# One 8 KB gather of both expert rows per slot, in place of two 4 KB gathers, in a decoder layer on one core

## The chip, the cores and the metric

The kernel runs on one core of a Trainium2 chip. The metric is the device time of one execution, in microseconds (us). Five engines of the core work side by side, each through its own instruction list in order: TensorE (PE, with its weight loads PEld), VectorE (DVE), ScalarE (ACT), GpSimd (POOL) and SyncE (SP). They wait for each other by semaphores. Sixteen DMA engines move data for transfers that the engines issue.

## What is computed

The reference is one layer of a decoder, for a prompt of 512 tokens and 8 sample tokens: three attention branches, their merge, and then a mixer of experts with product keys. The change lies in this mixer. Each token has 8 heads with 16 experts each, thus 128 slots. An expert is one row of 1024 numbers (4 KB) in each of two tables:

```
u = u_tab[e_idx]                    # (tokens, 128, 1024)
v = v_tab[e_idx]
a = gelu(einsum('tsd,td->ts', u, x)) * gate
y = h + einsum('ts,tsd->td', a, v)
```

The indices `e_idx` and the gates come from the retrieval, a search by scores.

## The kernel before

The 512 prompt tokens are 4 tiles of 128 tokens, a token per partition. The mixer (`mix_prompt`) runs over 4 x 128 = 512 slots; in a slot every partition needs the rows of its own expert. For slot s of tile t:

- POOL issues an indirect DMA of 128 rows of `u_tab` (L3190), 4 KB each, in all 0.5 MB, into one of six buffers. It waits till the product of slot s-6 is done.
- VectorE multiplies the row with the token and sums it up (L3219: two instructions, the product and a short read of the accumulator), into `ex_dots`.
- ScalarE takes the GELU of 16 slots at once (L3267, 128x16). VectorE multiplies 16 of them with the gates (L3226).
- POOL issues the rows of `v_tab` (L3199) 21 steps behind, into one of six other buffers. It waits till slot s-6 of these is used up.
- The row times the coefficient is added to y 24 steps behind (`LAG`), in one of two ways that `adds_on_vector` lays down by slot: on VectorE (L3235), or on TensorE (L3292) as a matmul with a diagonal matrix that ScalarE makes (L3262).

The rest of the layer runs beside these slots. A planner of fixed numbers (`RETRIEVE_HALF` to `MEMORY`, class `Beside`) spreads each stage evenly over a range of slot steps, on every engine: at step s an engine first issues what is due of the side stage, then its part of the slots. The stages are the retrieval for the other tiles (steps 0 to 62), the merge of the last two tiles (62 to 106), its output projection and norm (to 147), retrieval of the last tiles (to 211), weights (to 217), the compression of the sample cache (COMPRESS, 217 to 289, 256 loads `cs_ch` of 128 KB issued by SP), index and selection (to 353), then the attention of the samples with gathers by POOL (L2147, `da_kv`, `da_bias`, `sl_kv`, `sl_bias`), and the memory attention. Order and place are thus fixed; only the time at which a step comes moves. After the prompt block `expert_samples` does the same mixing for the 8 sample tokens, in 8 chunks of 128 rows (L3346 gathers, L3435 products, L3365 matmuls).

Of the kernel before, what the change touches and what calls it, by code (L numbers as in the profile page):

```python
# [15 lines left out]
P = 128  # L16
D = 1024
# [208 lines left out]
class Kernel:  # L226
# [1024 lines left out]
    def compress_samples(self, wts):  # L1251
# [7 lines left out]
        with tmp:  # L1259
# [43 lines left out]
            with self.block(COMPRESS) as block:  # L1303
# [113 lines left out]
                def _(dve):  # L1417
# [3 lines left out]
                    mix_done, acc_done = self.mix_sems[3][4:6]  # L1421
                    _, dve_upto, pe_upto = v_counts()
                    dve.wait_ge(mix_done, pe_upto[V_MOVES - 1])
                    dve.wait_ge(acc_done, dve_upto[V_MOVES - 1])
# [1242 lines left out]
    def finish_rows(self, tag, x_t, o_t, rows, load_x, h, xf, save=(), ahead=False, extra=(), early=False):  # L2667
# [5 lines left out]
        with tmp:  # L2673
# [22 lines left out]
            def turn(name, dst):  # L2696
                self.transposes(f"{tag}_{name}", [(dst[:, 4 * q:4 * q + 4, P * t:P * t + r], [mixed[:r, t, P * k:P * k + P] for k in range(4 * q, 4 * q + 4)])
                                                  for t, r in enumerate(rows) for q in range(2)])


            also = [(h[:r, t, :], load_x[t]) for t, r in enumerate(rows)] + list(extra)
# [4 lines left out]
            turn("mixed", t_view)  # L2706
# [4 lines left out]
            self.linear(f"{tag}_pq", t_view, rows, i["w_pq"], D, mixed, also=save, loaded=pq_w)  # L2711
# [7 lines left out]
    def finish_prompt(self, tag, t0, t1, h, o_t):  # L2719

        self.finish_rows(tag, self.xT[:, :, P * t0:P * t1], o_t, ROWS[t0:t1], self.xs[t0:t1], h, self.xf_prompt[:, t0:t1],
                         save=[(self.s["h"][P * t0:P * t1].rearrange("(t p) d -> p t d", p=P), h)], early=t0 == 0)
# [6 lines left out]
    def prompt_experts(self):  # L2729

        ctx = ExitStack()
        with ctx:
# [18 lines left out]

            u = lambda n: u_new[:, n % NU_BUF] if n % NU_BUF < NU_BUF // 2 else u_old[:, n % NU_BUF - NU_BUF // 2]
            work = ExitStack()
            with work:
# [3 lines left out]
                self.mix_sems = ([self.sem(f"ex_u_in{n}") for n in range(NU_BUF)], [self.sem(f"ex_v_in{n}") for n in range(NV_BUF)],  # L2758
                                 [self.sem(f"ex_h_in{n}") for n in range(2)],
# [6 lines left out]
            with work:  # L2766
                h = self.sb("fq_h", [P, TP - FIRST_TILES, D], F32, work)
                self.finish_prompt("fq", FIRST_TILES, TP, h[:], self.o_rest[:])
# [13 lines left out]
            self.mix_prompt(idx, gate, dots, coef, u=u, v=v, x=lambda t: self.xf_prompt[:, t], y=lambda t: y[:, t % 2], diag=diag, y_ps=y_ps,  # L2782
# [372 lines left out]
    def mix_prompt(self, idx, gate, dots, coef, u, v, x, y, diag, y_ps, chosen, beside, merged):  # L3155
# [4 lines left out]
        u_in, v_in, h_in, (dot_done, gelu_done, coef_done, diag_done, mix_done, acc_done, y_done) = self.mix_sems  # L3160
# [348 lines left out]
```

## Time and profile before

| what | us |
|---|---|
| median of three runs | 3009.91 (3000.89 to 3014.22) |
| span of the profiled execution, its first to its last instruction | 3030.2 |
| mixing of the prompt, first to last product | 812.8 to about 2832 |
| last addition into y of the prompt | 2893.9 |
| sample experts, first gather to the end | 2993.1 to 3030.2 |

Beside the span no other time is listed for the profiled execution; its span is 20.3 us above the median. The stages of the mixing phase, by the slot steps above, lie in the trace as: steps 0 to 41 from 812.8 to 923.3 us, 42 to 61 to 993.4, merge to 1189.8, projection and norm to 1347.5, compression 1566.9 to 1912.6, attention of the samples from 2170.1 (95 products to 2589.1), sliding-window attention of the samples to about 2830. The mixing takes two thirds of the time, and no engine is busy over more than 60% of the whole, so it is read by stage.

### The profile page before, as it was taken

The numbers are of one execution on the slowest core, as the hardware profiler recorded it, in microseconds if no ns is written. First come the engines' busy times: TensorE is split into PE (matmuls) and PEld (weight loads), VectorE is DVE, ScalarE is ACT, GpSimd is POOL, SyncE is SP. The second block draws the span as 40 slices with busy tenths as digits, with TensorE's granted clock in tenths as the row PEclk, the third lists the DMA queues.
The fourth block names the chain that finished last, engine by engine and source line by source line (L and its number), as shares of the span: only waits on it lengthen the run. The fifth ranks groups of instructions, "written<-read, shape, count | busy, mean of one in ns | idle before, by whom it ended". The sixth has DMA issues, their size and how long they took to land. (4 is left out here: it accounts for less than half of the span.)

```text
span 3030.2 us, 26401 instructions
## 1 busy us (share of the span) xinstructions
PE 1823.4 (60%) x7749; PEld 1077.9 (36%) x7749; DVE 1804.8 (60%) x3991; ACT 391.4 (13%) x994; POOL 1371.8 (45%) x1331
## 2 busy tenths in 40 slices
PE   7999796998145696456615645676212231655575
PEld 3475664544122232222204433552112221444521
DVE  4344556311688666679986656678566646766513
ACT  2010464301010001101100111111000010110000
POOL 1000242100267445567775443656567776755302
PEclk9999798999579798778967777558655555555577
DMA  4031400342389988999999997888678779977753
GB/s 137 23 115 37 169 2 1 111 153 104 111 283 351 361 323 288 330 356 354 338 348 370 335 328 274 310 287 314 198 242 316 255 248 339 344 272 279 278 211 112
DMA packets 273785, 727.80 MB, mean 240 GB/s; under 512 B 47881, under 2 KB 91426, under 8 KB 273066
## 3 DMA queue, kind: packets, MB, share of 16 engines
q0 software_dynamic: 156672, 564.61, 51.9%
q1 hardware_dynamic: 115802, 157.28, 15.0%
q10 hardware_dynamic: 1168, 4.23, 0.4%
q8 instruction: 62, 1.02, 0.1%
q14 instruction: 81, 0.66, 0.1%
HBM read 717.42 MB, written 12.66 MB: 241 GB/s over the span
## 5 line engine op out<-in xcount | busy, mean ns | idle before, releaser
L3199 POOL DMA_INDIRECT branch_rows_t<-in_v_tab,e_idx x437 | 519.8, 1190 | 400.5 <-DVE heads_t L3235 269.7
L3190 POOL DMA_INDIRECT ex_u<-in_u_tab,e_idx x257 | 279.0, 1086 | 350.2 <-POOLq L3093 246.7
L3235 DVE SCALAR_TENSOR_TENSOR heads_t<-branch_rows_t,ex_coef,heads_t 128x1024 f32<-128x1024 f32 x333 | 427.3, 1283 | 3.3 <-DVE me_lt L2648 0.3
L3219 DVE CUSTOM_DVE_ANT_0 ex_u<-ex_u,heads_t 128x1024 f32<-128x1024 f32 x257 | 314.1, 1223 | 168.8 <-DMA ex_u<-in_u_tab,e_idx 153.7
L3219 DVE CUSTOM_DVE_ANT_0 heads_t<-heads_t 128x1024 f32<-128x1024 f32 x255 | 311.9, 1224 | 132.2 <-DMA heads_t<-in_u_tab,e_idx 116.4
L3190 POOL DMA_INDIRECT heads_t<-in_u_tab,e_idx x255 | 276.1, 1083 | 88.5 <-issue 75.8
L3292 PE MATMUL ex_y_ps<-branch_rows_t,heads_t 128*128 128x512 f32 x416 | 215.3, 653 | 115.3 <-DMA branch_rows_t<-in_v_tab,e_idx 51.1
L1335 PE MATMUL cs_pp<-cs_ch,xn_t 128*128 128x256 f32 x512 | 139.0, 439 | 192.6 <-DMA cs_ch<-in_cache_cmp_kv 192.6
L818 PE MATMUL in_acc<-in_w,xn_t 128*128 128x512 f32 (+7 forms) x560 | 208.8, 529 | 6.0 <-POOLq L176 4.5
L1335 PEld LDWEIGHTS cs_pp<-cs_ch,xn_t 128*128 128x128 f32 x512 | 113.2, 224 | 220.5 <-DMA cs_ch<-in_cache_cmp_kv 142.8
L3292 PEld LDWEIGHTS ex_y_ps<-branch_rows_t,heads_t 128*128 128x128 f32 x416 | 79.0, 205 | 244.1 <-issue 173.2
L818 PEld LDWEIGHTS in_acc<-in_w,xn_t 128*128 128x128 f32 (+1 forms) x560 | 96.0, 176 | 108.9 <-issue 88.6
L1843 POOL IOTA heads_t<- 128x32 int32 x1 | 0.2, 164 | 223.1 <-SPq L175 223.1
L1936 PE MATMUL sl_at_lt_ps<-sample_q_t,sl_at_kt 64*128 64x4 f32 x256 | 64.8, 357 | 59.5 <-issue 44.8
L1636 PE MATMUL at_t_ps<-at_diag,at_exp 128*128 128x128 f32 (+3 forms) x608 | 87.4, 288 | 21.9 <-POOL at_diag L1724 21.1
L3199 POOL DMA_INDIRECT cmp_k_t<-in_v_tab,e_idx x50 | 61.9, 1237 | 73.9 <-DVE heads_t L3235 56.9
L3267 ACT ACTIVATE ex_coef<-ex_dots 128x16 f32<-128x16 f32 x32 | 6.9, 216 | 663.3 <-DVE ex_dots L3219 566.8
L1936 PEld LDWEIGHTS sl_at_lt_ps<-sample_q_t,sl_at_kt 64*128 64x128 f32 x256 | 59.2, 319 | 85.0 <-issue 69.3
L2865 PE MATMUL fq_mg_g_ps<-fq_mg_wg,xn_t 128*128 128x512 f32 x192 | 85.0, 595 | 0.0
L1636 PEld LDWEIGHTS at_t_ps<-at_diag,at_exp 128*128 128x128 f32 (+3 forms) x608 | 71.8, 185 | 34.8 <-POOL at_diag L1724 22.3
L1722 POOL TENSOR_SCALAR at_diag<-ident,at_sum,branch_gates 128x128 f32<-128x128 f32 x96 | 42.0, 447 | 74.4 <-DVE at_sum L1762 68.7
L1678 ACT ACTIVATE at_exp<-at_logits,at_max 128x128 f32<-128x128 f32 (+7 forms) x128 | 63.0, 493 | 65.1 <-DVE at_max L1750 63.9
(715 smaller groups left out, 3190.8 us busy)
## 6 DMA issues: line engine op xcount, KB each, us to landing
cs_ch<-in_cache_cmp_kv SPq DMA_DIRECT2D x256, 128.0 KB
fq_mg_wg<-in_w_gate SPq DMA_DIRECT2D x6, 2048.0 KB, 18.3
in_w<-in_w_in SPq DMA_DIRECT2D x4, 2048.0 KB
branch_rows_t<-in_v_tab,e_idx POOLq DMA_INDIRECT x437
first_w<-in_w_gate SPq DMA_DIRECT2D x3, 2048.0 KB, 7.9
fp_wb<-in_w_branch SPq DMA_DIRECT2D x6, 1024.0 KB, 10.2
fp_wg<-in_w_gate SPq DMA_DIRECT2D x3, 2048.0 KB, 8.1
fq_mg_wb<-in_w_branch SPq DMA_DIRECT2D x6, 1024.0 KB, 22.0
```

The source lines that it names most:

```text
L818: last = pe.matmul(acc[:r, u % 2, :n], self.xT[:, k, P * t:P * t + r], w[:, j % 2, k, :n], start=(k == 0), stop=(k == KD - 1))
L1335: last = pe.matmul(pp[:, n % 2, 256 * c:256 * c + 256].rearrange("p (g k m) -> p g k m", g=KV, m=8), wts[:, c, r, :], ch[:, n % NBUF, :, c ...
L1636: last = pe.matmul(t_ps[:w, u % 2, k, :], ex[:, u % 6, P * k:P * k + w], diag[:, u % 4, :], start=True, stop=True)
L1678: act.activation(ex[:, u % 6, :keys(u)], src[:, u % 4, :keys(u)], ACT.Exp, bias=mx[:, u:u + 1], scale=scale, accum_out=sm[:, u:u + 1]).the ...
L1722: pool.tensor_scalar(d, ident[:], r, self.g_nsa[:, t, k:k + 1], ALU.mult, ALU.mult).then_inc(scaled, 1)
L1936: last = pe.matmul(ltv[:m, g, j, b, :], lhs, q, start=True, stop=True)
L2865: last = pe.matmul(g_ps[:r, u % 2, :], xT[:, k, cols], wg[j % depth][:, k, :], start=(k == 0), stop=(k == KD - 1))
L3190: pool.indirect_dma_start(out=u(s), out_offset=None, in_=i["u_tab"], in_offset=bass.IndirectOffsetOnAxis(ap=idx[:, t, m:m + 1], axis=0)).t ...
L3199: pool.indirect_dma_start(out=v(n), out_offset=None, in_=i["v_tab"], in_offset=bass.IndirectOffsetOnAxis(ap=idx[:, t, m:m + 1], axis=0)).t ...
L3219: dve.tensor_tensor_reduce(out=u(s), in0=u(s), in1=x(t), scale=1.0, scalar=0.0, op0=ALU.mult, op1=ALU.add, accum_out=dots[:, t, m:m + 1]). ...
L3235: dve.scalar_tensor_tensor(out=y(t), in0=v(n), scalar=coef[:, t, m:m + 1], in1=y(t), op0=ALU.mult, op1=ALU.add).then_inc(acc_done, 1)
L3292: last = pe.matmul(y_ps[:, q, :], diag[:, (pe_upto[n] - 1) % 8], v(n)[:, 512 * q:512 * q + 512], start=n in first_pe, stop=n in last_pe)
```

## The change

Both tables become one, `uv_tab`, a row of 8 KB: 1024 numbers of u, then 1024 of v. The host puts them side by side. A slot has one gather of 128 rows of 8 KB, 1 MB (L3201 after), into one of seven buffers of 8 KB; it waits till slot s-7 has both its product and its addition. The lag of the additions falls from 24 steps to 3. ScalarE makes the coefficient slot by slot at the next step: a GELU of 128x1 (L3257), a wait for itself, a copy scaled by the gate (L3259), and for TensorE's slots the diagonal matrix. VectorE's product with the gates is gone. VectorE takes first the addition of slot s-3, then the product of slot s. As the rule in `adds_on_vector` goes by step, other slots fall to TensorE: 162 where it was 134, and 350 to VectorE where it was 378. The residual rows `fq_h` of the merged tiles, whose place is needed, are loaded between merge and projection. The sample experts have 8 gathers of 8 KB rows instead of 8 and 8.

```diff
-V_MOVES = 150
-NU_BUF = NV_BUF = 6
-CHUNK, LAG, AHEAD, SETTLE, RELOAD = 16, 24, 3, 4, 30
+ROW_MOVES = 172
+NBUF, NDIAG = 7, 4
+LAG, SETTLE, RELOAD = 3, 4, 30
...
+            old_pairs = self.heads_space(TP * D + 2 * D, [2, 2 * D])
+            diag = self.heads_space(TP * D + 6 * D, [NDIAG, P])
+            new_pairs = self.sb("ex_pairs", [P, 2, 2 * D], F32, ctx)
...
-                        if s >= NU_BUF:
-                            pool.wait_ge(dot_done, s - NU_BUF + 1)
-                        pool.indirect_dma_start(out=u(s), out_offset=None, in_=i["u_tab"],
-                                                in_offset=bass.IndirectOffsetOnAxis(ap=idx[:, t, m:m + 1], axis=0)).then_inc(u_in[s % NU_BUF], 16)
-                    n = s - LAG + AHEAD
...
-                        if n >= NV_BUF:
-                            mixed(pool, n - NV_BUF)
-                        pool.indirect_dma_start(out=v(n), out_offset=None, in_=i["v_tab"],
...
+                        if s >= NBUF:
+                            pool.wait_ge(dot_done, s - NBUF + 1)
+                            if by_dve[s - NBUF]:
+                                pool.wait_ge(acc_done, dve_upto[s - NBUF])
+                            else:
+                                pool.wait_ge(mix_done, pe_upto[s - NBUF])
+                        pool.indirect_dma_start(out=pair(s), out_offset=None, in_=i["uv_tab"],
+                                                in_offset=bass.IndirectOffsetOnAxis(ap=idx[:, t, m:m + 1], axis=0)).then_inc(pair_in[s % NBUF], 16)
...
-                    c = s - 3 - CHUNK
-                    if c >= 0 and c % CHUNK == 0 and c < NS:
-                        t, m = at(c)
-                        dve.wait_ge(gelu_done, c // CHUNK + 1)
-                        w = coef[:, t, m:m + CHUNK]
-                        dve.tensor_tensor(w, w, gate[:, t, m:m + CHUNK], ALU.mult).then_inc(coef_done, 1)
...
-                    n = s - LAG + AHEAD
-                    if 0 <= n < NS and not by_dve[n]:
...
-                    if s % CHUNK == CHUNK - 1 and s < NS:
...
+                    n = s - 1
+                    if 0 <= n < NS:
+                        t, m = at(n)
+                        c = coef[:, t, m:m + 1]
+                        act.wait_ge(dot_done, n + 1)
+                        act.activation(c, dots[:, t, m:m + 1], ACT.Gelu_apprx_tanh).then_inc(gelu_done, 1)
+                        act.wait_ge(gelu_done, n + 1)
+                        act.activation(c, c, ACT.Copy, scale=gate[:, t, m:m + 1]).then_inc(coef_done, 1)
+                        if not by_dve[n]:
+                            act.wait_ge(coef_done, n + 1)
+                            if pe_upto[n] > NDIAG:
+                                act.wait_ge(mix_done, pe_upto[n] - NDIAG)
+                            act.activation(diag[:, (pe_upto[n] - 1) % NDIAG], ident[:], ACT.Copy, scale=c).then_inc(diag_done, 1)
...
-                    for dst, table, sems in ((u, i["u_tab"], u_in), (rows, i["v_tab"], v_in)):
-                        for n in range(N):
-                            pool.indirect_dma_start(out=dst[:, n], out_offset=None, in_=table,
+                    for n in range(N):
+                        pool.indirect_dma_start(out=pairs[:, n], out_offset=None, in_=i["uv_tab"],
```

In the fence the pieces stand in the order of POOL, VectorE and ScalarE in `mix_prompt`, then POOL in `expert_samples`.

How the order moves shows at three places. First POOL, where the attention of the samples gathers its biases (`da_bias`); `ex_u`, `heads_t`, `branch_rows_t` and `ex_pairs` are places of the row buffers. Before:

```order
L3199 DMA branch_rows_t<-in_v_tab,e_idx 128x1024
L2147 DMA da_bias<-tmp_bias_pos,da_past_ix 128x16
L3190 DMA ex_u<-in_u_tab,e_idx 128x1024
L3199 DMA branch_rows_t<-in_v_tab,e_idx 128x1024
L2147 DMA da_bias<-tmp_bias_pos,da_past_ix 128x16
```

And after:

```order
L2147 DMA da_bias<-tmp_bias_pos,da_past_ix 128x16
L3201 DMA branch_rows_t<-in_uv_tab,e_idx 128x2048
L2147 DMA da_bias<-tmp_bias_pos,da_past_ix 128x16
L3201 DMA ex_pairs<-in_uv_tab,e_idx 128x2048
L2147 DMA da_bias<-tmp_bias_pos,da_past_ix 128x16
```

Where POOL issued two gathers of rows and one of biases to a step, it issues one and one.

Then ScalarE where the sliding-window attention copies its transposed keys (`sl_at_kt`, L1999) out of TensorE's memory. Before:

```order
L1999 COPY da_at_kt<-da_at_kt_ps 64x256 x3
L3267 ACT_TABLE_LOAD
L3267 ACTIVATE ex_coef<-ex_dots 128x16
L1999 COPY da_at_kt<-da_at_kt_ps 64x256 x13
L2002 ACT_TABLE_LOAD
L2002 ACTIVATE da_at_p,da_at_sm<-da_at_p,da_at_mx 64x264
L3267 ACT_TABLE_LOAD
L3267 ACTIVATE ex_coef<-ex_dots 128x16 x2
L1999 COPY sl_at_kt<-sl_at_kt_ps 64x256 x25
L3267 ACTIVATE ex_coef<-ex_dots 128x16
```

And after:

```order
L1999 COPY sl_at_kt<-sl_at_kt_ps 64x256
L3257 ACTIVATE ex_coef<-ex_dots 128x1
L3259 ACTIVATE ex_coef<-ex_coef,e_gate 128x1
L1999 COPY sl_at_kt<-sl_at_kt_ps 64x256 x2
L3257 ACTIVATE ex_coef<-ex_dots 128x1
L3259 ACTIVATE ex_coef<-ex_coef,e_gate 128x1
L1999 COPY sl_at_kt<-sl_at_kt_ps 64x256 x2
```

Up to 25 copies stood between two GELUs of 16 slots; now one or two copies stand between the coefficients of neighbouring slots.

Third, ScalarE in the compression, where `cs_hid` (L1395) waits for a matmul of TensorE. Before:

```order
L3267 ACTIVATE ex_coef<-ex_dots 128x16
L1322 COPY cs_part<-cs_pp 128x2x128 x2
L1395 ACTIVATE cs_hid<-cs_hp,cmp_peh 128x2x255
L1322 COPY cs_part<-cs_pp 128x2x128 x2
L1400 ACT_TABLE_LOAD
```

And after:

```order
L3257 ACTIVATE ex_coef<-ex_dots 128x1
L3259 ACTIVATE ex_coef<-ex_coef,e_gate 128x1
L1395 ACTIVATE cs_hid<-cs_hp,cmp_peh 128x2x255
L3257 ACTIVATE ex_coef<-ex_dots 128x1
L3259 ACTIVATE ex_coef<-ex_coef,e_gate 128x1
L3257 ACTIVATE ex_coef<-ex_dots 128x1
L3259 ACTIVATE ex_coef<-ex_coef,e_gate 128x1
L1322 COPY cs_part<-cs_pp 128x2x128 x2
```

Behind the waiting `cs_hid` stood coefficients that were up to 8 steps away from their use; now those of the next slot stand there.

## Rows read from the trace of the kernel before

**Rows 1.** the page's fifth part (groups of instructions), whole execution.
```profile
L3199 POOL DMA_INDIRECT branch_rows_t<-in_v_tab,e_idx x437 | 519.8, 1190 | 400.5 <-DVE heads_t L3235 269.7
...
L3235 DVE SCALAR_TENSOR_TENSOR heads_t<-branch_rows_t,ex_coef,heads_t 128x1024 f32<-128x1024 f32 x333 | 427.3, 1283 | 3.3 <-DVE me_lt L2648 0.3
L3219 DVE CUSTOM_DVE_ANT_0 ex_u<-ex_u,heads_t 128x1024 f32<-128x1024 f32 x257 | 314.1, 1223 | 168.8 <-DMA ex_u<-in_u_tab,e_idx 153.7
L3219 DVE CUSTOM_DVE_ANT_0 heads_t<-heads_t 128x1024 f32<-128x1024 f32 x255 | 311.9, 1224 | 132.2 <-DMA heads_t<-in_u_tab,e_idx 116.4
```

**Rows 2.** busy us (count) of PE, PEld, DVE, ACT, POOL; clock, DMA, GB/s.
```profile
812.80:923.30 110.50, 45.48 (x116) 19.36 (x116) 93.27 (x310) 14.27 (x36) 80.19 (x64) 0.71 0.85 299
923.30:993.40 70.10, 34.87 (x69) 12.28 (x68) 60.04 (x139) 5.14 (x14) 51.74 (x43) 0.88 0.92 331
993.40:1189.80 196.40, 171.51 (x400) 64.41 (x400) 118.33 (x155) 20.20 (x29) 90.30 (x85) 0.93 0.89 326
1189.80:1347.50 157.70, 71.92 (x199) 35.57 (x200) 108.45 (x142) 15.15 (x29) 96.11 (x86) 0.70 0.95 352
1566.90:1912.60 345.70, 169.47 (x676) 132.34 (x676) 209.22 (x369) 35.37 (x56) 165.53 (x150) 0.74 0.89 323
2170.10:2589.10 419.00, 92.08 (x800) 76.26 (x801) 254.29 (x402) 17.58 (x37) 296.71 (x271) 0.50 0.81 276
2589.10:2680.20 91.10, 53.04 (x207) 37.89 (x206) 77.99 (x99) 12.18 (x34) 70.93 (x65) 0.50 0.98 368
```

**Rows 3.** the same view, VectorE's product line L3219 alone.
```profile
812.80:923.30 110.50, 51.26 (x84) 0.71 0.85 299
...
2170.10:2589.10 419.00, 117.36 (x191) 0.50 0.81 276
```

**Rows 4.** POOL's groups of instructions, 2170.1 to 2589.1 us.
```profile
L3199 POOL DMA_INDIRECT branch_rows_t<-in_v_tab,e_idx x96 | 118.4, 1233 | 41.7 <-issue 28.1 <-DVE heads_t L3235 13.6
L3190 POOL DMA_INDIRECT heads_t<-in_u_tab,e_idx x48 | 49.6, 1033 | 14.6 <-issue 14.6
L3190 POOL DMA_INDIRECT ex_u<-in_u_tab,e_idx x49 | 48.0, 980 | 21.3 <-issue 21.3
```

**Rows 5.** VectorE's waits in it: us in total, times, longest.
```profile
DVE heads_t L3219 <- DMA heads_t<-in_u_tab,e_idx: 74.5, 38, 12.0
DVE ex_u L3219 <- DMA ex_u<-in_u_tab,e_idx: 67.1, 37, 5.3
```

**Rows 6.** queues, 1603 to 1621 us: packets, MB, share of 16 engines.
```profile
q0 software_dynamic: 1559, 5.68, 80.7%
q1 hardware_dynamic: 1559, 1.42, 23.0%
```

**Rows 7.** the same, 2811 to 2830 us.
```profile
q1 hardware_dynamic: 240, 6.82, 83.2%
q0 software_dynamic: 265, 1.01, 13.0%
```

**Rows 8.** the same, 1850 to 1856 us.
```profile
q1 hardware_dynamic: 880, 0.80, 43.8%
```

**Rows 9.** waits, 806 to 2880 us, VectorE's and ScalarE's.
```profile
DVE cs_part L1322 <- PE cs_pp L1335: 90.7, 8, 15.7
...
DVE ex_coef L3226 <- ACT ex_coef L3267: 20.5, 1, 20.5
...
ACT cs_hid L1395 <- PE cs_hp L1346: 155.4, 8, 27.4
...
ACT fq_mg_sig L2887 <- PE fq_mg_g_ps L2865: 87.7, 12, 9.7
```

**Rows 10.** the timeline at the end (start us, us).
```profile
2993.05 0.94 POOL L3346 DMA_INDIRECT es_u<-in_u_tab,es_idx  x1 [17.09 <-DVE es_idx L3426]
...
3011.39 15.27 PE L3365 MATMUL es_y_ps<-es_rows,es_diag 128*8 128x512 f32 x32 [25.08 <-ACT es_diag L3381]
```

**Rows 11.** the timeline of VectorE at 2893 us.
```profile
2893.46 0.19 DVE L2665 COPY sample_o_t<-me_o_ps 128x32 f32<-128x32 f32 x1 [20.35 <-PE me_o_ps L2633]
```

More of the change, by code:

```diff
@@ L2665, in _, with finish_rows @@
                     c.link(dve.tensor_copy(self.o8_t[:, 8:12, :], ov))
-    def finish_rows(self, tag, x_t, o_t, rows, load_x, h, xf, save=(), ahead=False, extra=(), early=False):
+    def finish_rows(self, tag, x_t, o_t, rows, load_x, h, xf, save=None, ahead=False, extra=(), early=False, late=False):
         nt, i = len(rows), self.i
@@ L2694, in finish_rows, with turn @@
             mixed = self.sb(f"{tag}_mixed", [P, nt, D], F32, tmp)
-            def turn(name, dst):
+            def turn(name, dst, store=None):
                 self.transposes(f"{tag}_{name}", [(dst[:, 4 * q:4 * q + 4, P * t:P * t + r], [mixed[:r, t, P * k:P * k + P] for k in range(4 * q, 4 * q + 4)])
-                                                  for t, r in enumerate(rows) for q in range(2)])
-            also = [(h[:r, t, :], load_x[t]) for t, r in enumerate(rows)] + list(extra)
+                                                  for t, r in enumerate(rows) for q in range(2)], store=store)
+            also = ([] if late else [(h[:r, t, :], load_x[t]) for t, r in enumerate(rows)]) + list(extra)
             if ahead:
@@ L2705, in finish_rows, with load_h @@
                 self.merge(tag, x_t, o_t, rows, mixed, also, weights=weights, after=after, samples=not early)
-            turn("mixed", t_view)
+            load_h = None
+            if late:
+                h, h_in = self.sb(f"{tag}_h", [P, nt, D], F32, tmp)[:], self.sem(f"{tag}_h_in")
+                def load_h(sp):
+                    for t, r in enumerate(rows):
+                        sp.dma_start(h[:r, t, :], load_x[t]).then_inc(h_in, 16)
+                    sp.wait_ge(h_in, 16 * nt)
+            turn("mixed", t_view, load_h)
             self.linear(f"{tag}_out", t_view, rows, i["w_out"], D, h, add=h, loaded=out_w, ahead=then)
@@ L2766, in prompt_experts @@
             with work:
-                h = self.sb("fq_h", [P, TP - FIRST_TILES, D], F32, work)
-                self.finish_prompt("fq", FIRST_TILES, TP, h[:], self.o_rest[:])
+                self.finish_prompt("fq", FIRST_TILES, TP, None, self.o_rest[:], late=True)
             self.recycle()
@@ L3331, in expert_samples @@
             y_ps = self.ps("es_y_ps", [P, 2, 512], ctx)
-            u_in = [self.sem(f"es_u_in{n}") for n in range(N)]
-            v_in = [self.sem(f"es_v_in{n}") for n in range(N)]
+            pair_in = [self.sem(f"es_pair_in{n}") for n in range(N)]
             stored = self.stores("y_sample")
@@ L3362, in _ @@
                         pe.wait_ge(diag_done, n + 1)
-                        pe.wait_ge(v_in[n], 16)
+                        pe.wait_ge(pair_in[n], 16)
                         for a in range(2):
-                            last = pe.matmul(y_ps[:DB, a, :], diag[:, n, :], rows[:, n, 512 * a:512 * a + 512], start=(n == 0), stop=(n == N - 1))
+                            last = pe.matmul(y_ps[:DB, a, :], diag[:, n, :], pairs[:, n, D + 512 * a:D + 512 * a + 512], start=(n == 0), stop=(n == N - 1))
                     last.then_inc(mix_done, 1)
@@ L3474 @@
     for name in _INS:
+        if name == "v_tab":
+            continue
+        if name == "u_tab":
+            put("uv_tab", _np.concatenate([_np.asarray(inputs["u_tab"]), _np.asarray(inputs["v_tab"])], axis=1))
+            continue
         a = _np.ascontiguousarray(inputs[name])
```

84 lines of the change are left out of this document (34 added, 50 removed).

## The prediction

> **What bounds the kernel now.** I read the groups of instructions first. VectorE's products wait for their rows: 153.7 us in one group of buffers and 116.4 in the other [rows 1], 270 us together, a tenth of the span. POOL's v gathers wait most for VectorE's additions, 269.7 us; that is a full ring, not a shortage. So the question is what makes the u rows late, and the busy shares by stretch answer it differently by stage [rows 2]:
>
> - Steps 0 to 61 (812.8 to 993.4 us): VectorE is busy 93.27 of 110.5 and 60.04 of 70.1 us, with the retrieval between its products. VectorE bounds.
> - Merge (993.4 to 1189.8): TensorE 171.51 of 196.4 us. TensorE bounds.
> - Projection and norm (1189.8 to 1347.5) and 2589.1 to 2680.2: the DMA engines at 0.95 and 0.98, 352 and 368 GB/s. Bytes bound.
> - Compression (1566.9 to 1912.6): nobody is over 0.89; VectorE waits 90.7 us for `cs_pp` [rows 9], and that waits for the 128 KB loads.
> - 2170.1 to 2589.1: DMA only at 0.81 and 276 GB/s, VectorE 254.29 of 419 us, POOL 296.71 in 271 instructions. Here stand 74.5 + 67.1 = 141.6 us of the 270 [rows 5]. POOL's own groups show idle time put down to "issue" behind nearly every gather, 14.6 us for 48 and 21.3 for 49 [rows 4]: with some 0.3 us between 271 instructions, about 80 us, and 296.71 busy, POOL is occupied 378 of 419 us. POOL bounds, by the number of its gathers.
>
> **The change part by part.** The sum is made against the profiled span of 3030.2 us, which lies 20.3 us above the median of the runs; I take the same 20.3 off at the end.
>
> *POOL in the attention of the samples.* Each of 97 steps loses a u gather: 49.6 + 48.0 busy and 14.6 + 21.3 of issue gaps [rows 4] = 133 us of POOL. The row that remains is priced as a v gather now, 1233 ns, since it too is one descriptor list of 128 rows. POOL would then need 419 - 133 = 286 us. VectorE needs 254.29 plus its waits for others than rows, so at least 254. The bytes stay: 419 us at 276 GB/s [rows 2] are 115.6 MB, which take 314 us at 368 GB/s, the best rate of a long stretch [rows 2], or 293 us at 7.10 MB in 18 us = 394 GB/s, the best of a short one [rows 6]. So the DMA is next, and the gain is at most 127 us and at least nothing. The mean rate of the four stretches at 0.89 or more [rows 2] is (326 + 352 + 323 + 368) / 4 = 342; that is where this kernel arrives when it asks for all it can. 115.6 / 0.342 = 338: **-81**.
>
> The Trainium skill (DMA: Bandwidth & Descriptors, section Anatomy of one DMA — SWDGE (gpsimd) path) fits a transfer from POOL as some 2.0 us plus its bytes at 436 GB/s, and its section Bandwidth advises at least 1 MiB. By that, two 0.5 MB transfers cost 6.4 us and one of 1 MB 4.4, an estimate from that page; it would give 2 us for every slot wherever rows are waited for. The rows that are gathered now speak against this here: with 0.5 MB gathers the engines already reach 0.98 and 368 GB/s [rows 2], so this start is covered by transfers in flight.
>
> *Head.* A product needed 0.5 MB; now it needs its whole pair. Up to 923.3 us 84 / 2 = 42 products ran (the count takes in the reads of the accumulator) [rows 3], and only 18 v rows were due, so 110.5 us at 299 GB/s = 33 MB sufficed. Now 42 pairs are 42 x 1.05 = 44 MB, and at 350 GB/s (the projection's 352 [rows 2]) that takes 126 us: **+16**. Bounds: nothing (394 GB/s would give 112) to +37 (at 299). The next 20 steps need 21 MB, 60 us, under VectorE's 70: nothing. In the merge, TensorE's slots are added no faster and no slower; its bound stays: nothing, bounds -5 to +10 for the packets that weights now queue with.
>
> *Longer packets.* From the two windows a packet costs a + b x bytes: 1559 packets of 3.64 KB in 0.807 x 16 x 18 us = 149 ns [rows 6], 240 of 28.4 KB in 0.832 x 16 x 19 us = 1054 ns [rows 7]. So b = 0.0365 ns per byte and a = 16 ns; a pair in one packet saves 16 of 298 ns, 5%, at most (window 6 counts 103.9% in all, so the true a is smaller). I take 3% on 157.7 + 91.1 = 249 us [rows 2]: **-8**, bounds 0 to -13.
>
> *Compression.* It is fed by 256 loads of 128 KB in 1 KB pieces. Beside gathers both queues moved 1559 packets each [rows 6]: one of theirs for one of the others', 1.42 MB in 18 us = 79 GB/s for `cs_ch`, and 133 GB/s when alone [rows 8]. With pieces of 8 KB against 1 KB the same turn gives it 1 part in 9, about 44 GB/s. 256 x 131 KB = 33.6 MB at 44 GB/s would take 763 us, but only while a gather is under way; the total of bytes is the same, and the ring holds the gathers back when VectorE waits. One bound is nothing. For the other: between 79 and 44 GB/s a load of 131 KB takes 1.7 or 3.0 us, 1.3 more; if a sixth of the 256 are met when they are waited for, 54 us. I take the lower end's neighbourhood, as VectorE's wait for `cs_pp` is only 90.7 us in 8: **+10**.
>
> *ScalarE and the short lag.* The gate product leaves VectorE: 32 short instructions, inside a stretch where it waits anyway: nothing. Two small activations per slot come to ScalarE, each at most the 0.2 us or so of other rows: 0.4 of a slot that lasts 2.8 us or more, at ACT busy 17.58 of 419 [rows 2]. The coefficient is now due two steps later instead of eight or more. Against it stands one gain: VectorE waited 20.5 us for the GELU that stood behind 25 copies [rows 9]; a stage that waits for its transposed keys will keep half: **-10**, bounds -20 to 0. Additions: 28 move from VectorE to TensorE at 1283 ns [rows 1], but 24 of all stood behind the last product, where the end is set by the memory attention: `me_o_ps` is what VectorE waits 20.35 us for at 2893.46 [rows 11]. Shorter tail: nothing.
>
> *Sample experts.* TensorE's 32 matmuls take 15.27 us from 3011.39 [rows 10] and need the coefficients of all 8 products. Eight pairs of 1.05 MB from 2993.05 + 2 at 350 GB/s land at 3019, where eight u rows sufficed before: the end moves by some 10 us: **+10**, bounds +4 to +14.
>
> Sum: -81 + 16 - 8 + 10 - 10 + 10 = **-63**, so 2967 in the profile and 3009.9 - 63 = 2947, say **2945** in the runs.
>
> **The rivals.**
>
> *B, ScalarE in lockstep (slower).* ScalarE waits for TensorE in its side stages: 155.4 us in 8 for `cs_hp`, 87.7 in 12 for the merge's gates [rows 9]. Before, a coefficient behind such a wait had 8 steps; now VectorE's additions have two steps, about 5 us, then VectorE stops, so does the ring, and TensorE's next work for VectorE is late too. It decides from 78 us on, the 63 of the gain and the 15 that a measurement needs. If 15 us of each of the 8 waits fall on VectorE, 120 are lost: 3009.9 - 63 + 120 = about 3067. Against it: VectorE waits in the same stage for the same TensorE already (90.7), and ScalarE's waits are partly its running ahead. Chance 0.14.
>
> *C, queues share badly (no change).* Weights of merge and projection, `cs_ch` and the samples' rows queue in turn with 8 KB packets; +54 in the compression instead of 10 and +10 in the merge, so 2945 + 54 = about 3000. Chance 0.12.
>
> *D, POOL's price grows with the row.* If 128 rows of 8 KB cost POOL twice the 1233 ns, the gain of 81 goes: 3009.9 - 63 + 81 = 3028. No row has such a gather; that POOL writes one list entry for each row, whatever its length, is my assumption, and v and u rows of one length differ by 0.2 us already [rows 4]. Chance 0.05.
>
> *E, the fixed start of a transfer.* Each row wait was the start of a transfer, and a transfer fewer gives nearly all 270 us back, less the head and the end: 3010 - 270 + 16 + 10 = about 2766. The section cited above would have it so. Chance 0.06.
>
> **How the numbers follow.** My own case has 0.63; its own range is 2901 to 2991, from the largest bound taken alone on either side (-127 for -81, +54 for +10). With E below and B above, each cut off in part, the range of 8 in 10 is 2893 to 3032: it leaves out most of E and most of B. Faster, by over 0.5% (what a measurement of this kernel can tell from no change; under 2995): my case, E and 0.03 of C, 0.72. Within: 0.09 of C and 0.03 of D, 0.12. Slower: B and 0.02 of D, 0.16.
>
> **What the changed profile would show.** The POOL line of gathers near 1.2 us each in the stretch with `da_bias`, the stretch at 340 to 370 GB/s and about 340 us instead of 419, product waits there under 60 us. The 42nd product about 16 us later after the first. `cs_pp` waits some 10 us longer. Few waits of VectorE's addition for L3259; many over 5 us mean B. A gather of 2.4 us on POOL means D. The prediction is wrong if the stretch from 2170 on stays at 276 GB/s, or if additions wait for coefficients by over 60 us in all.

## The result, and the profile after

The changed kernel takes 2871.69 us (median of 4 runs, 2866.79 to 2881.74) where the kernel before took 3012.06 in the same rounds. The ratio is 0.957, with a 95% interval of 0.951 to 0.963. The forecast was 2945, with a range of 2893 to 3032. It is faster by 140 us, twice the 65 that I had given it, and outside the range.

The profiled span is 2873.5 us against 3030.2, so 157 us less. That is 17 more than the medians differ by, since the profiled execution of before lies above its median; in which stages these 17 stand can't be told. A second profile of the changed kernel (experiment 12) has each stage within 6 us of the one shown, but for the compression (356.6 us). The time between the starts of two products gives it by stage. The forecast beside it is that of my sum:

| steps | what runs beside | before, us | after, us | change | forecast |
|---|---|---|---|---|---|
| 0 to 62 | retrieval | 180.6 | 178.8 | -2 | +16 |
| 62 to 106 | merge | 196.4 | 207.5 | +11 | 0 |
| 106 to 147 | projection, norm | 157.7 | 166.5 | +9 | -5 |
| 147 to 217 | retrieval, last | 219.3 | 210.4 | -9 | 0 |
| 217 to 289 | compression | 345.7 | 347.4 | +2 | +10 |
| 289 to 353 | index, selection | 257.6 | 230.7 | -27 | 0 |
| 353 to 448 | attention of the samples | 418.9 | 330.3 | -89 | -81 |
| 448 to 480 | sliding window, first part | 91.1 | 81.0 | -10 | -3 |
| 480 to 511 | sliding window, second part | 150.7 | 103.8 | -47 | -10 |
| from 511 on | memory attention, sample experts | 199.4 | 203.4 | +4 | +10 |

The groups of instructions of the page after, which answer to [rows 1]:

```profile
L3201 POOL DMA_INDIRECT ex_pairs<-in_uv_tab,e_idx x147 | 188.4, 1281 | 543.1 <-POOLq L3099 244.1
L3201 POOL DMA_INDIRECT branch_rows_t<-in_uv_tab,e_idx x171 | 210.1, 1229 | 283.3 <-DVE heads_t L3226 183.7
...
L3231 DVE CUSTOM_DVE_ANT_0 branch_rows_t<-branch_rows_t,heads_t 128x1024 f32<-128x1024 f32 x171 | 208.8, 1222 | 58.9 <-DMA branch_rows_t<-in_uv_tab,e_idx 55.5
...
L3231 DVE CUSTOM_DVE_ANT_0 ex_pairs<-ex_pairs,heads_t 128x1024 f32<-128x1024 f32 x147 | 179.8, 1223 | 47.1 <-DMA ex_pairs<-in_uv_tab,e_idx 44.7
L3231 DVE CUSTOM_DVE_ANT_0 heads_t<-heads_t 128x1024 f32<-128x1024 f32 x146 | 178.1, 1221 | 42.0 <-DMA heads_t<-in_uv_tab,e_idx 39.2
...
L3259 ACT ACTIVATE ex_coef<-ex_coef,e_gate 128x1 f32<-128x1 f32 x512 | 150.8, 294 | 16.6
```

A gather of 8 KB rows takes POOL 1229 to 1281 ns, where a v gather of 4 KB rows took 1190. The products wait 55.5 + 44.7 + 39.2 = 139 us for their rows in these three groups, where it was 270. The stretches, with the columns of [rows 2]:

```profile
813.60:929.20 115.60, 85.55 (x197) 33.47 (x198) 94.94 (x309) 42.62 (x133) 62.75 (x41) 0.91 0.93 382
929.20:992.40 63.20, 38.24 (x72) 13.25 (x71) 60.52 (x139) 19.65 (x60) 29.95 (x19) 0.86 0.88 360
992.40:1199.90 207.50, 171.21 (x400) 64.38 (x400) 117.42 (x153) 62.06 (x131) 51.18 (x44) 0.91 0.81 313
1199.90:1366.50 166.60, 72.51 (x198) 35.70 (x199) 105.75 (x141) 35.55 (x110) 47.44 (x41) 0.69 0.85 331
1576.80:1924.20 347.40, 165.86 (x676) 129.05 (x676) 207.09 (x365) 67.73 (x194) 95.94 (x79) 0.74 0.86 322
2155.00:2485.30 330.30, 81.98 (x803) 67.85 (x804) 251.80 (x396) 62.27 (x222) 192.43 (x174) 0.51 0.91 350
2485.30:2566.30 81.00, 75.67 (x299) 55.08 (x299) 77.70 (x97) 29.30 (x113) 41.98 (x32) 0.50 1.01 420
```

From 2155 to 2485 us POOL is busy 192 us in 174 instructions, where it was 297 in 271; VectorE fills 252 of 330 us, and the bytes flow at 350 GB/s instead of 276. From 2485 to 2566 VectorE is busy 77.7 and TensorE 75.7 of 81 us, and the DMA engines are full at 420 GB/s: three limits lie close together there now (experiment 8 takes the bytes away and leaves 75). In the merge TensorE still needs 171 us, and the stretch is 11 us longer. POOL's gathers from 2155 to 2485 us, as in [rows 4]:

```profile
L3201 POOL DMA_INDIRECT branch_rows_t<-in_uv_tab,e_idx x41 | 46.1, 1123 | 51.6 <-DVE heads_t L3226 25.9 <-DVE ex_dots L3231 17.2 <-issue 8.5
L3201 POOL DMA_INDIRECT ex_pairs<-in_uv_tab,e_idx x28 | 33.6, 1201 | 15.6 <-DVE heads_t L3226 8.9 <-issue 6.4 <-DVE ex_dots L3231 0.3
L3201 POOL DMA_INDIRECT heads_t<-in_uv_tab,e_idx x28 | 32.1, 1145 | 24.9 <-DVE heads_t L3226 18.0 <-issue 6.9
```

97 gathers, 1123 to 1201 ns each, and most of the idle time before them, 70 of 92 us, is now the full ring (VectorE's addition or product), no longer "issue". Three waits of VectorE over the mixing, as in [rows 9]:

```profile
DVE cs_part L1322 <- PE cs_pp L1335: 66.8, 7, 17.6
...
DVE cmp_v L1432 <- PE cs_op L1358: 31.2, 4, 21.1
...
DVE heads_t L3226 <- ACT ex_coef L3259: 3.7, 12, 0.3
```

The addition waited 3.7 us in all for a coefficient. In the compression the wait for `cs_pp` is shorter than before (90.7) and that for `cs_op` longer (2.3 before). At the end, the first gather of the sample experts and TensorE's last matmuls, as in [rows 10]:

```profile
2827.20 0.95 POOL L3341 DMA_INDIRECT es_pairs<-in_uv_tab,es_idx  x1 [17.34 <-DVE es_idx L3421]
```

```profile
2853.20 16.72 PE L3360 MATMUL es_y_ps<-es_pairs,es_diag 128*8 128x512 f32 x32 [32.73 <-ACT es_diag L3376]
```

From the first gather to the end it is 46.3 us, where it was 37.2.

### The profile page after: what moved, and what is told of

Read it like the earlier page. It is cut to its first block and busy times, and to the rows that moved or that the text cites. A ratio compares the mean times of both kernels' runs of the same rounds, so it can differ in the third digit from the quotient of the medians.

```text
span 2873.5 us, 27584 instructions
## 1 busy us (share of the span) xinstructions
PE 1869.8 (65%) x7861; PEld 1083.5 (38%) x7861; DVE 1762.6 (61%) x3931; ACT 673.3 (23%) x2034; POOL 845.4 (29%) x811
## 5 line engine op out<-in xcount | busy, mean ns | idle before, releaser
L3257 ACT ACTIVATE ex_coef<-ex_dots 128x1 f32<-128x1 f32 x512 | 103.5, 202 | 1124.4 <-DVE ex_dots L3231 1006.4
L3201 POOL DMA_INDIRECT ex_pairs<-in_uv_tab,e_idx x147 | 188.4, 1281 | 543.1 <-POOLq L3099 244.1
L3201 POOL DMA_INDIRECT branch_rows_t<-in_uv_tab,e_idx x171 | 210.1, 1229 | 283.3 <-DVE heads_t L3226 183.7
L3201 POOL DMA_INDIRECT heads_t<-in_uv_tab,e_idx x146 | 183.5, 1257 | 284.8 <-DVE heads_t L3226 182.9
L3231 DVE CUSTOM_DVE_ANT_0 branch_rows_t<-branch_rows_t,heads_t 128x1024 f32<-128x1024 f32 x171 | 208.8, 1222 | 58.9 <-DMA branch_rows_t<-in_uv_tab,e_idx 55.5
L3231 DVE CUSTOM_DVE_ANT_0 ex_pairs<-ex_pairs,heads_t 128x1024 f32<-128x1024 f32 x147 | 179.8, 1223 | 47.1 <-DMA ex_pairs<-in_uv_tab,e_idx 44.7
L3231 DVE CUSTOM_DVE_ANT_0 heads_t<-heads_t 128x1024 f32<-128x1024 f32 x146 | 178.1, 1221 | 42.0 <-DMA heads_t<-in_uv_tab,e_idx 39.2
L3226 DVE SCALAR_TENSOR_TENSOR heads_t<-branch_rows_t,ex_coef,heads_t 128x1024 f32<-128x1024 f32 x126 | 161.6, 1282 | 10.8 <-DMA is_w<-tmp_w 5.6
L3259 ACT ACTIVATE ex_coef<-ex_coef,e_gate 128x1 f32<-128x1 f32 x512 | 150.8, 294 | 16.6
L3226 DVE SCALAR_TENSOR_TENSOR heads_t<-heads_t,ex_coef 128x1024 f32<-128x1024 f32 x100 | 128.1, 1281 | 27.5 <-issue 23.4
L3226 DVE SCALAR_TENSOR_TENSOR heads_t<-ex_pairs,ex_coef,heads_t 128x1024 f32<-128x1024 f32 x100 | 128.1, 1281 | 5.1 <-DMA fq_ffn_gain<-in_ln_ffn 0.9
L3289 PEld LDWEIGHTS ex_y_ps<-ex_pairs,heads_t 128*128 128x128 f32 x188 | 37.3, 215 | 150.3 <-ACT heads_t L3264 117.6
## 6 DMA issues: line engine op xcount, KB each, us to landing
fp_wb<-in_w_branch SPq DMA_DIRECT2D x6, 1024.0 KB, 10.4
```

The source lines that it names most:

```text
L3201: pool.indirect_dma_start(out=pair(s), out_offset=None, in_=i["uv_tab"], in_offset=bass.IndirectOffsetOnAxis(ap=idx[:, t, m:m + 1], axis=0 ...
L3226: dve.scalar_tensor_tensor(out=y(t), in0=v(n), scalar=coef[:, t, m:m + 1], in1=y(t), op0=ALU.mult, op1=ALU.add).then_inc(acc_done, 1)
L3231: dve.tensor_tensor_reduce(out=u(s), in0=u(s), in1=x(t), scale=1.0, scalar=0.0, op0=ALU.mult, op1=ALU.add, accum_out=dots[:, t, m:m + 1]). ...
L3257: act.activation(c, dots[:, t, m:m + 1], ACT.Gelu_apprx_tanh).then_inc(gelu_done, 1)
L3259: act.activation(c, c, ACT.Copy, scale=gate[:, t, m:m + 1]).then_inc(coef_done, 1)
L3289: last = pe.matmul(y_ps[:, q, :], diag[:, (pe_upto[n] - 1) % NDIAG], v(n)[:, 512 * q:512 * q + 512], start=n in first_pe, stop=n in last_pe)
```

## The experiments

The time before differed between the chips that the runs came to (3006 to 3025 us), so each ratio is to runs of the kernel before on the same chip. The changed kernel itself came to 0.957 on one chip and 0.949 on another, so ratios of different chips can't be told apart below about 1%.

### 1. The pairing undone, all else kept

```diff
-                        pool.indirect_dma_start(out=pair(s), out_offset=None, in_=i["uv_tab"],
-                                                ...).then_inc(pair_in[s % NBUF], 16)
+                        for half, table, sems in ((u, i["u_tab"], pair_in), (v, i["v_tab"], v_in)):
+                            pool.indirect_dma_start(out=half(s), out_offset=None, in_=table,
+                                                    ...).then_inc(sems[s % NBUF], 16)
```

> The kernel after, but each slot has two gathers of 4 KB rows again (u rows, then v rows, each with its own semaphore) into the two halves of the same ring of seven; lag 3, order and ScalarE's work as after. Theory P (the gain is the pairing: half the gathers on POOL, and 8 KB packets that move more bytes per second): the stretch of steps 353 to 448 goes back from 330 us to 400 to 430, and the whole is 2970 to 3030. Theory S (the short lag and ScalarE's coefficients slot by slot made most of the gain): at most 2930, and that stretch under 370.

Measured: 3021.05 us, ratio 1.005 (1.002 to 1.009). The stretch of steps 353 to 448:

```profile
2191.20:2607.70 416.50, 87.81 (x813) 73.73 (x813) 254.59 (x396) 62.33 (x222) 307.14 (x272) 0.50 0.82 280
```

POOL is busy 307 us in 272 instructions and the stretch takes 416 us, nearly that of before. Lag 3, the one ring of seven and ScalarE's coefficients are worth nothing together without the pairing: theory P. They are not neutral stage by stage, though. Steps 0 to 42 take 135.7 us (110.5 before) and 147 to 211 218.8 (202.2), which I read as u gathers that can no longer run ahead of their v rows; steps 480 to 511 take 117.5 instead of 150.7. So of the 47 us gained in that last stage 33 come from the rest of the change, and 14 more with the pairing. VectorE's longest wait left in it is for TensorE:

```profile
DVE sample_o_t L2058 <- PE sl_at_o_ps L1986: 17.9, 1, 17.9
```

### 2. ScalarE's coefficients alone

```diff
-                        act.activation(coef[:, t, c], dots[:, t, c], ACT.Gelu_apprx_tanh).then_inc(gelu_done, 1)
+                        act.activation(c, dots[:, t, m:m + 1], ACT.Gelu_apprx_tanh).then_inc(gelu_done, 1)
+                        act.wait_ge(gelu_done, n + 1)
+                        act.activation(c, c, ACT.Copy, scale=gate[:, t, m:m + 1]).then_inc(coef_done, 1)
```

> The kernel before (two gathers, lag 24), with only the coefficient made slot by slot on ScalarE as after, and without the product with the gates on VectorE. Theory P: 2960 to 3005, and what is gained lies in steps 480 to 511 (150.7 us before, 103.8 after), where VectorE waited for the GELU behind the copies. Theory S: at most 2940, with gains in several stages.

Measured: 3032.09 us, ratio 1.010 (1.005 to 1.016). Both theories had expected less time, and both are wrong here: this part alone costs about 1%. Steps 480 to 511 took 154.7 us. VectorE's longest waits in them:

```profile
DVE sl_at_lt L2012 <- PE sl_at_o_ps L1954: 37.3, 1, 37.3
DVE ex_u L3219 <- DMA ex_u<-in_u_tab,e_idx: 19.9, 7, 15.6
```

The wait of 20.5 us for the GELU behind its copies [rows 9] is gone, and 37.3 us of waiting for TensorE's sliding-window matmuls stand in its place (7.0 before). TensorE had lost time there that the profile puts down to nothing it names ("issue"), 28.7 us where it was 10.4 before; the section on the hardware comes back to it:

```profile
PE sl_at_lt_ps L1936 <- issue: 28.7, 4, 7.6
```

### 3 and 4. POOL's time given back without bytes

```diff
+                        for n in range(4):
+                            if s or n:
+                                pool.wait_ge(self.padded, 4 * s + n)
+                            pool.memset(self.pad[:], 0.0).then_inc(self.padded, 1)
```

> The kernel after, with four small memsets (128x256, some 0.3 us each) on POOL behind each gather, which give POOL back about the 1.4 us per slot that the second gather took, and move no bytes. If POOL's issue time was what held steps 353 to 448: that stretch goes from 330 to about 400 us and the whole to 2930 to 2970. If instead the length of the packets made the gain there: the stretch stays within 10 us and the whole at 2870 to 2890.

Measured with four memsets: 3016.38 us, ratio 1.003 (1.000 to 1.006). Then with two of them:

> The kernel after with two small memsets on POOL behind each gather instead of the four of the run before it (four made 3016 us where 2872 stood; in the trace they took 1.44 us a slot and 0.15 between). If POOL's time sets the pace step by step, there is a point below which it costs nothing: 0.72 + 0.15 us a slot bring steps 353 to 448 from 330 to 345 to 365 us, and the whole to 2890 to 2930, less than half of the 144 of four. If the memsets do harm in another way (a port, a semaphore), half of them cost half: 2935 to 2955.

Measured with two: 2898.48 us, ratio 0.9585 (0.953 to 0.964), that of the changed kernel within the interval. Steps 353 to 448, four and two memsets:

```profile
2187.30:2582.20 394.90, 78.30 (x805) 64.29 (x805) 255.97 (x396) 62.31 (x222) 318.23 (x554) 0.50 0.82 292
```

```profile
2167.20:2525.20 358.00, 78.30 (x805) 64.30 (x805) 254.96 (x395) 62.30 (x222) 278.50 (x367) 0.50 0.88 323
```

The bytes and their 8 KB packets were those of after in both. 318 us of POOL made the stretch 395 us long, 278 made it 358, 192 make it 330. The run with two met its forecast in the stretch (345 to 365) and in the whole (2890 to 2930). By the ratios (0.957 and 0.949 without, 0.9585, 1.003) the first half of the load costs between nothing and 1%, by the stretch 28 us, and the second half 4.5%: a bound, not an equal tax for each memset. That the whole gain was lost with four exceeded my 2930 to 2970. The load was somewhat above that of the second gather (106.6 us in steps 448 to 480, 91.1 before), and POOL bounded in more stages than I had counted: 210.2 us in steps 147 to 211 (196.2 after), 114.7 in 289 to 317 (100.3), 121.8 in 480 to 511 (103.8).

### 5. The rows alone

56 gathers of pairs, then 56 of u and 56 of v, ahead of the first slot, while no engine computes:

```diff
+            for n in range(56):
+                gather(2 * (n % NBUF), pair(n % NBUF), i["uv_tab"], n)
...
+            for n in range(56):
+                gather(2 * (n % NBUF), u(n % NBUF), i["u_tab"], n)
+                gather(2 * (n % NBUF) + 1, v(n % NBUF), i["v_tab"], n)
```

> The kernel after, with the disputed transfers by themselves ahead of the first slot, while VectorE waits: 56 gathers of 8 KB rows through the ring of seven, and when all are there 56 pairs of gathers of 4 KB rows of the same experts. 58.7 MB each. Packets matter: 8 KB at 400 GB/s or more, 4 KB at 375 or less, both with the DMA engines over 0.95. Packets don't matter: both within 3% in rate, or the 4 KB ones held by POOL's 112 issues of 1.3 us with the DMA share under 0.95.

The stretches of the two, pairs first, from one execution:

```profile
805.00:945.80 140.80, 0.00 (x0) 0.00 (x0) 0.00 (x0) 0.00 (x0) 50.24 (x54) 0.50 1.01 418
949.00:1095.40 146.40, 0.00 (x0) 0.00 (x0) 0.00 (x0) 0.00 (x0) 103.58 (x111) 0.50 1.01 401
```

418 GB/s against 401. Long packets give 4% at most: the 8 KB gathers waited for their rows to land, but of the 4 KB ones none waited for a buffer. There POOL issued one every 1.24 us without a pause, 139 of the 146 us, so its issues may have held that rate although the DMA share reads 1.01. My 3% is neither confirmed nor refuted. But 4 KB rows reached 401 GB/s here, where the stage that I had called bound by bytes stood at 368 [rows 2]. A gather took POOL 0.94 us and 0.30 us of gap with either length. The Trainium skill (DMA: Bandwidth & Descriptors, section Anatomy of one DMA — SWDGE (gpsimd) path) gives each such transfer a fixed 2.0 us; laid end to end, 56 transfers of 4.4 us would take 246 us by that estimate, where 141 were measured. With seven under way that start is covered, as the rows of before had shown.

### 6 and 7. The lead and the lag

Only `LAG` is changed, 2 or 4 instead of 3.

> The kernel after with LAG 2 instead of 3: gathers start five slots ahead of their product instead of four, the coefficient is due a step sooner. If what remains of the waits for rows is a lead too short, the whole is 2835 to 2865, with the gain in steps 353 to 448. If ScalarE then becomes late, VectorE's addition waits for the copy with the gate and it is 2880 to 2950.

Measured with LAG 2: 2865.92 us, ratio 0.9495 (0.943 to 0.956).

> The kernel after with LAG 4: gathers start three slots ahead, the coefficient is due a step later. If the lead matters: 2885 to 2930. If the lead is long enough and ScalarE's lateness matters: 2850 to 2870.

Measured with LAG 4: 2882.90 us, ratio 0.953 (0.947 to 0.959). The intervals of 2, 3 and 4 overlap. But 2 and 4 ran on the same chip, four times each: 2853 to 2877 us against 2875 to 2886, 16 us apart in the mean, at the edge of what so few runs can tell. The products' waits for rows went up with the lag in the profiles (122 us in three groups with 2, 139 with 3, 200 with 4); of these 78 us about 16 show in the time. With 2, steps 353 to 448 took 320.2 us, 10 less than with 3. ScalarE was not late with 2: the addition waited 3.7 us in all for it, as with 3.

### 8. Half the bytes

The v rows are left out: the addition takes the product's buffer instead.

```diff
-            return pair(n)[:, D:]
+            return pair(n)[:, :D]
...
-                        pool.indirect_dma_start(out=pair(s), out_offset=None, in_=i["uv_tab"],
+                        pool.indirect_dma_start(out=u(s), out_offset=None, in_=i["u_tab"],
```

> The kernel after, with one gather per slot of 4 KB rows of u only; the addition takes the product's buffer in place of the v row, so the v rows are left out. As many gathers as after, packets of 4 KB, half the bytes. If the stalls of TensorE between matmuls of sl_at_o_ps (31.2 us in 37 gaps before, none after) come from 4 KB packets, they are back, 15 us or more; if from the number of gathers that POOL issues, there are none. If bytes bound after's steps 353 to 480 they fall from 411 to 370 us or less, the whole to 2740 to 2800; if VectorE and the samples' chain bound them, the whole stays over 2830.

Measured: 2733.85 us, ratio 0.904 (0.899 to 0.910). Steps 353 to 480 took 387 us instead of 411: half the bytes take only 6% off, so bytes alone don't bound them (353 to 448 take 312.1 us, 448 to 480 take 74.9); VectorE's 252 of 330 and 77.7 of 81 us of work stay. The 139 us of the whole lie in many stages where rows and weights share the queues: 17 in steps 0 to 42, 12 in 62 to 84, 11 each in 106 to 122 and 122 to 147, 25 in 217 to 241. So bytes are worth more after the change than any one stage shows.

### 9. A second gather that moves next to nothing

```diff
+                        pool.indirect_dma_start(out=self.few[:, 16 * (s % NBUF):16 * (s % NBUF) + 16], out_offset=None, in_=i["few"],
+                                                in_offset=...).then_inc(self.few_in[s % NBUF], 16)
```

> The kernel after, and behind each gather of 8 KB rows POOL issues a second one of 64 B rows (128x16) from a small table: two gathers a slot as before, the bytes of after. TensorE's unexplained idle time over the mixing (251 us before, 306 with two 4 KB gathers, 66 after, 26 with the memsets): if it comes from the number of gathers or of their packets, 200 us or more; if from POOL's being occupied or from 4 KB packets, under 80. The time by POOL's occupation alone (about 1.3 us more a slot): 2950 to 3010.

Measured: 3061.21 us, ratio 1.011 (1.007 to 1.014). Steps 353 to 448:

```profile
2212.10:2626.60 414.50, 86.45 (x804) 72.46 (x804) 253.87 (x395) 62.30 (x222) 296.59 (x270) 0.50 0.79 281
```

POOL's 297 us in 270 instructions are those of before (297 in 271), and so is the stretch: 414.5 against 419.0 us, with the packets and the bytes of after. So what the second gather carries doesn't matter; that there is one makes the stage. The 3061 us are more than the 2950 to 3010 that I had put for POOL's occupation alone. The memsets say the same: they kept POOL busy longer (318 us), and the stretch was still 20 us shorter (394.9). Of the 84 us that a second gather costs here, POOL's being occupied thus explains some 65. What makes the other 20 is open. One thing differs: over these steps TensorE's waits put down to "issue" come to 95 us here, 54 in the changed kernel and none with the memsets. That this makes the 20 us was not shown.

### 10 to 12. The sample experts, and a last try

The sample experts' u and v rows are gathered apart again (10), with `LAG` 2 besides (11), and the changed kernel ran once more beside them (12).

> The kernel after, with the sample experts' rows in 8 gathers of u and 8 of v again. If the pairing there delays the last product, as the sum had it: 7 to 11 us less than after on the same chip, and from the first such gather to the end 37 us instead of 46. If not: no change.

> The run before this one with LAG 2 too. If a lead of five slots is worth what the run with LAG 2 alone looked like (5 to 20 us under after): 12 to 28 us less than after. If that was noise: 7 to 11 us less, as the run before this one.

> The kernel after, unchanged, for comparison with the two runs above on the same chip; 2865 to 2895, 0.95 to 0.963 of before.

Measured: 2872.09 us (0.949, 0.945 to 0.953), 2863.21 (0.947, 0.943 to 0.951) and 2866.61 (0.949, 0.944 to 0.953). In the profiles the last part shrinks as forecast, from 46.1 us from its first gather to the end to 37.1 and 37.0. In the time of the whole it doesn't show: the intervals are 12 us wide to either side, so a gain of 9 us is neither shown nor excluded. With LAG 2 besides, it is 3 us under run 12, where 12 to 28 had been forecast for a lead that matters. No version tried is clearly better than the changed kernel.

## Why the prediction was wrong

**The direction and the main term held.** Steps 353 to 448 were to gain 81 us and gained 89, and the second gather on POOL is the cause: taken away it makes 330 us, its time given back by memsets 395, by gathers 414. That the size came out so near is in part luck. The sum stopped at 338 since bytes at 342 GB/s were to be the next bound, but with half the bytes the stretch still takes 312 us, so bytes are in the main not what holds it at 330. (Five stretches of [rows 2] are at 0.89 or more, not four; with the fifth the mean is 340 and the term -79.) The price of an 8 KB gather on POOL was that of a v gather, so rival D is out.

**The step that failed is the price of the stages outside steps 353 to 448.** By the profiles the change is 157 us where the sum has 63. Of the 94 us between them 64 lie in two terms: steps 480 to 511, put at 10 and measured at 47, and steps 289 to 353, put at nothing without a row and measured at 27. A further 7 lie in steps 448 to 480, where the bound was misread, and 9 in 147 to 217, put at nothing.

*The misread bound.* I read 2589.1 to 2680.2 us as "bytes bound" from a DMA share of 0.98. POOL's groups in that stretch of the kernel before:

```profile
L3199 POOL DMA_INDIRECT branch_rows_t<-in_v_tab,e_idx x32 | 40.2, 1255 | 10.4 <-issue 9.2 <-DVE heads_t L3235 1.3
L3190 POOL DMA_INDIRECT ex_u<-in_u_tab,e_idx x18 | 16.9, 940 | 5.5 <-issue 5.5
L3190 POOL DMA_INDIRECT heads_t<-in_u_tab,e_idx x15 | 14.4, 958 | 4.6 <-issue 4.6
```

That is 71.5 us busy and 19.3 of gaps between issues: POOL was occupied 90.8 of 91.1 us. After the change the same steps ran at 420 GB/s. By the sum that I made for one stretch (busy time plus 0.3 us for each instruction) from the rows that I had, 1189.8 to 1347.5 comes to 122 of 158 us, but 812.8 to 993.4 to 164 of 181. I made that sum for a single stage. Retrieval in steps 147 to 211 is another such stage: 156.4 us busy in 128 instructions, thus 195 of 202. But it doesn't hold for the two terms that missed most. The stretches of steps 480 to 511 and of 289 to 317, before:

```profile
2680.20:2830.90 150.70, 81.58 (x715) 67.28 (x716) 82.59 (x131) 14.65 (x35) 69.58 (x62) 0.50 0.72 272
...
1912.60:2028.80 116.20, 86.99 (x375) 78.76 (x376) 85.69 (x147) 11.36 (x22) 68.52 (x70) 0.50 0.86 311
```

POOL was occupied 88 of 151 and 90 of 116 us by the same sum, so it did not hold them. Experiment 3 says what the second gather's time on POOL costs all over: its place filled by memsets, the span is 3006.7 us instead of 2873.5, 133 of the 157 us, and the ratio of the runs (1.003) leaves nothing of the gain. Of these 65 lie in steps 353 to 448, and 26 + 18 + 14 + 14 in steps 448 to 480, 480 to 511, 147 to 211 and 289 to 317, where my sum had 3 + 10 + 0 + 0. The memsets were somewhat dearer than the gather, and in the faster kernel POOL comes to its limit sooner, so these are upper ends.

*The last stage.* I gave steps 480 to 511 half of one wait, 10 us with a bound of 20; they gained 47. Three waits of VectorE in them, before:

```profile
DVE ex_coef L3226 <- ACT ex_coef L3267: 20.5, 1, 20.5
...
DVE sample_o_t L2058 <- PE sl_at_o_ps L1986: 16.1, 1, 16.1
DVE sl_at_lt L2012 <- PE sl_at_o_ps L1954: 7.0, 1, 7.0
```

All three are gone after, 43.6 us; the last two are named nowhere in my sum. Experiment 1 puts 33 us on the rest of the change and 14 on the pairing. In it the first and the third wait are gone (27.5 us), and the second stands at 17.9: with the pairing that one goes too. The coefficients alone don't do it (experiment 2, +4), since TensorE is late there instead. Which of the shorter lag, the order of addition and product and the other slots on TensorE keeps it in time was not tried apart, and stays open.

*Steps 289 to 353* gained 12 us in experiment 1 as well, so about half of their 27 isn't the pairing. Two waits of VectorE in them are gone after, and all but 0.8 us of them in experiment 1:

```profile
DVE is_relu L2242 <- remote: 11.9, 3, 6.9
DVE is_kt L2252 <- remote: 9.2, 3, 6.7
```

What they wait for the profile doesn't name; the cause stays open.

**The head** was to lose 16 and lost 5 up to step 42, and won 7 in the next 20: pairs came at 382 GB/s, where I had put the 350 of another stage. Again a rate that a stage had was taken for the rate that it could have.

**Smaller terms.** Compression +2, and +11 in the second profile of the changed kernel, for +10. The mechanism of rival C is there: in the window from 1603 to 1621 us of the changed kernel the two queues moved 900 and 899 packets, and the loads of `cs_ch` came at 0.82 MB in 18 us, 46 GB/s, near the 44 of the prediction. But its price of 54 us did not come. Merge, projection and norm lost 20 us together where I had -5. Against before they lose 20 in the changed kernel, 10 with four memsets, 12 with the small gather, 4 with two gathers of 4 KB, and with half the bytes they gain 15: that fits rival C, weights that share the queues with rows, in a small size. It was not tried by itself. The sample experts' end is 9 us longer in the profile, as forecast. ScalarE in lockstep (B) cost 3.7 us in waits of the addition in all, though the copy with the gate took 294 ns where I had put 0.2 us. E, a fixed start given back with each transfer, would have had 2766; the rows waited for fell by 131 us, but the small gather that adds a transfer per slot and the memsets that add none both lose the gain, so the start of a transfer is not its cause.

The range was too narrow since no bound in it stood for a stage that the sum had left out or priced by one wait: steps 289 to 353 and 480 to 511 together gained 74 us, where my sum had 10.

## What to carry to other kernels

Add the gaps between its issues to the busy time of an engine that issues DMAs, in every stage, before a DMA share near 1 is read as a bound by bytes: here 1.0 to 1.2 us of busy time came with 0.3 us of gap, and half a megabyte each made a share of 0.98 at 368 GB/s, and the same steps ran at 420 afterwards. Where one engine issues every row gather, tables that are read by the same index belong side by side. A bound that is relieved frees each stage that it held, so price it in each, and read each stage's other waits too, even where no row of the changed part stands in them: they made most of the miss here.

## What the runs showed of the hardware

TensorE stalls between matmuls that wait for nothing the profile names ("issue"). The same 384 matmuls of the sliding-window attention, before, 131 of them in one run and then stalls of up to 1.14 us every few, and after:

```profile
2750.41 7.42 PE L1986 MATMUL sl_at_o_ps<-sl_at_pt,sl_kv 128*64 128x2 f32 x131
...
2769.63 0.40 PE L1986 MATMUL sl_at_o_ps<-sl_at_pt,sl_kv 128*64 128x2 f32 x4 [1.05 <-issue]
2771.07 0.30 PE L1986 MATMUL sl_at_o_ps<-sl_at_pt,sl_kv 128*64 128x2 f32 x3 [1.03 <-issue]
2771.81 0.41 PE L1986 MATMUL sl_at_o_ps<-sl_at_pt,sl_kv 128*64 128x2 f32 x5 [0.45 <-issue]
2772.57 0.42 PE L1986 MATMUL sl_at_o_ps<-sl_at_pt,sl_kv 128*64 128x2 f32 x4 [0.34 <-issue]
```

```profile
2605.91 20.65 PE L1986 MATMUL sl_at_o_ps<-sl_at_pt,sl_kv 128*64 128x2 f32 x384
```

They take 48 us before and 20.65 after. TensorE's waits put down to "issue", over the mixing of the kernel before and of the run with the small second gather:

```profile
PE sl_at_lt_ps L1936 <- issue: 44.8, 19, 5.6
...
PE sl_at_o_ps L1986 <- issue: 21.0, 35, 1.1
```

```profile
PE wi_at_lt_ps L1936 <- issue: 33.4, 14, 20.8
...
PE sl_at_o_ps L1986 <- issue: 22.6, 34, 2.0
```

Summed over all lines from 806 us on they are 251 us before, 306 with two 4 KB gathers, 284 with the coefficients alone and 209 with the small second gather; with one gather a slot they are 66 and 85 (changed kernel, twice), 26 and 17 (four and two memsets), 64 with half the rows. These sums hold single gaps of up to 52 us as well. The stalls under 1.5 us alone come to 66 to 85 us in 102 to 131 pieces in the four kernels with two gathers a slot, and to 6 to 23 us in 10 to 36 pieces in those with one. So they go with the number of gathers that POOL issues (or of the rows in them, 128 each: the two were not told apart), not with its being occupied, nor with the length of the packets. This had not been expected. How a gather of POOL holds up TensorE's instructions is not shown. What it costs can be estimated: the small gather loads POOL no more than the four memsets do, and the two stand 0.8% apart by their ratios (1.011 and 1.003), some 23 us, which is near what the difference between two chips can be.
